# A two-block fp32 transformer kernel: the second block's streams and output products with sequence positions on the partitions

## What is computed

```python
for layer in range(DEPTH):                      # DEPTH = 2
    xm = modulate(h, g_pre_m, sh_m, sc_m)       # rms_norm_2(x, g) * (1 + scale) + shift
    cm = modulate(hc, g_pre_m, csh_m, csc_m)
    y, yc = even_mixer(...) or odd_mixer(...)   # each ends in ... @ w_out
    h = h + gt_m * rms_norm_2(y, g_post_m)
    f = conv_ffn(modulate(h, g_pre_f, sh_f, sc_f), w_up[layer], conv_w[layer], conv_b[layer], w_down[layer])
    h = h + gt_f * rms_norm_2(f, g_post_f)
    # layer 0 does the same two steps for hc
def conv_ffn(x, w_up, conv_w, conv_b, w_down):
    h = conv_over_sequence(x @ w_up) + conv_b   # 3 taps, each channel apart
    a, g = jnp.split(h, 2, axis=-1)
    return (jax.nn.silu(g) * a) @ w_down
```

## Time and profile before

| | us |
|---|---|
| median of three runs | 2123.23 |
| the three runs | 2123.23, 2120.9, 2126.95 |
| the profiled execution | 2119.83 |
| its span in the trace | 2117.8 |
| mean granted TensorE clock in it | 0.967 of full speed |

### The profile page before, as it was taken

The page is one execution under the profiler, slowest core; times in us unless marked ns, Lnnn a source line. Parts: engine busy times, 40 slices in busy tenths (PEclk is TensorE's granted clock), DMA queues, the critical chain, the costliest instruction groups (busy, mean ns, idle before and its releaser), DMA issues.

```text
span 2117.8 us, 33330 instructions
## 1 busy us (share of the span) xinstructions
PE 1988.5 (94%) x14346; PEld 1793.4 (85%) x14346; DVE 1186.1 (56%) x1541; ACT 948.9 (45%) x1294; POOL 12.9 (1%) x17
## 2 busy tenths in 40 slices
PE   6999889999999998899999989899999979979997
PEld 6998867998899887699979878788889978569997
DVE  5555774545544568654555473565553366746764
ACT  5434534434533453443455364543333255645553
POOL 0000000000000000000000100000000000000000
PEclk9999978999999999799999999899999999989998
DMA  7665534665466554476443220232232212023551
GB/s 284 251 219 199 179 126 153 249 229 210 168 233 233 210 174 174 151 271 239 148 162 117 100 80 21 73 104 102 81 101 97 100 60 97 24 80 117 183 192 68
DMA packets 45072, 320.90 MB, mean 152 GB/s; under 512 B 4992, under 2 KB 5120, under 8 KB 6400
## 3 DMA queue, kind: packets, MB, share of 16 engines
q1 hardware_dynamic: 38160, 270.09, 36.1%
q10 hardware_dynamic: 6768, 48.69, 6.2%
HBM read 317.72 MB, written 1.05 MB: 151 GB/s over the span
## 4 chain that ended last, share of the span: by engine, by line
PE 84%; DVE 8%; ACT 4%; issue 3%; DMA 0%; SPq 0%; DVEq 0%; ACTq 0%
PE ps L476 82%; DVE s_wl L1723 2%; ACT s_wh L1125 2%; DVE s_big L1993 1%; PE ps L769 1%; DVE s_tmp L2156 1%; ACT s_tmp L1401 1%; DVE s_tmp L1735 0%; PE ps L632 0%; DMA s_ca<-in_c_all 0%; PE ps L731 0%; DVE s_tmp L2112 0%; ACT s_xh L1404 0%; DVE s_X L1883 0%; ACT s_xh L1125 0%
## 5 line engine op out<-in xcount | busy, mean ns | idle before, releaser
L476 PE MATMUL ps<-s_xh,s_wl 128*128 128x256 f32 (+1 forms) x2400 | 734.2, 306 | 29.4 <-DVE s_wl L1723 15.8
L476 PE MATMUL ps<-s_xl,s_wh 128*128 128x256 f32 (+1 forms) x2400 | 725.7, 302 | 0.0
L476 PE MATMUL ps<-s_xh,s_wh 128*128 128x256 f32 (+1 forms) x2400 | 725.6, 302 | 0.0
L1723 DVE TENSOR_TENSOR s_wl<-s_raw,s_wh 128x2048 fp32r<-128x2048 f32 x215 | 492.3, 2291 | 404.3 <-ACT s_wh L1125 404.1
L476 PEld LDWEIGHTS ps<-s_xh,s_wl 128*128 128x128 f32 x2400 | 463.5, 193 | 50.0 <-DVE s_wl L1723 15.8
L1125 ACT ACTIVATE s_wh<-s_raw 128x2048 fp32r<-128x2048 f32 x215 | 409.5, 1906 | 191.0 <-PE ps L476 190.6
L476 PEld LDWEIGHTS ps<-s_xl,s_wh 128*128 128x128 f32 x2400 | 463.7, 193 | 15.6
L476 PEld LDWEIGHTS ps<-s_xh,s_wh 128*128 128x128 f32 x2400 | 463.1, 193 | 15.7
L476 PE MATMUL ps<-s_hh,s_wl 128*128 128x256 f32 x528 | 149.8, 284 | 0.0
L476 PE MATMUL ps<-s_hl,s_wh 128*128 128x256 f32 x528 | 149.4, 283 | 0.0
L476 PE MATMUL ps<-s_hh,s_wh 128*128 128x256 f32 x528 | 149.4, 283 | 0.0
(11 more groups left out here) (207 smaller groups left out, 2783.5 us busy)
## 6 DMA issues: line engine op xcount, KB each, us to landing
s_big<-in_w_ada ACTq DMA_DIRECT2D x46, 1024.0 KB, 6.6
s_raw<-in_ffn_gate SPq DMA_DIRECT2D x44, 1024.0 KB, 6.4
s_raw<-in_ffn_up SPq DMA_DIRECT2D x44, 1024.0 KB, 5.0
s_raw<-in_ffn_down SPq DMA_DIRECT2D x44, 1024.0 KB, 5.0
s_raw<-in_w_up SPq DMA_DIRECT2D x44, 1024.0 KB, 4.9
s_raw<-in_w_down SPq DMA_DIRECT2D x22, 1024.0 KB, 4.9
s_raw<-in_w_in SPq DMA_DIRECT2D x18, 1024.0 KB, 4.9
s_raw<-in_w_in_ab SPq DMA_DIRECT2D x10, 1024.0 KB, 4.9
```

Source lines behind the costliest of these rows:

```text
L476: return pe.matmul(o, lhsT, rhs, start=start, stop=stop, skip_group_check=True)
L1723: dve.tensor_tensor(wide(wl, u), raw[:, u % SLOTS, :].rearrange("p (k n) -> p k n", k=8), f32(wide(wh, u)), SUB).then_inc(*w_low.tick(u))
```

## The change

- **Layout.** The streams (`Xs`) and the products of output projection and conv down (`Ys`) have positions on the partitions: [128, 2, 1024]. The root mean square of a position is then a number of its partition.
- **Output projection** goes through `tokens`, in four pieces of 256 channels as before. **Conv down** (`conv_down`) takes the hidden stream as the stationary operand and 512 channels of a weight as columns: 8 x 3 products a step. The order of steps is the same.
- **Norms.** `bound_stat`, `bound_spread`, the sums and diagonals of squares are gone. ACT's Square accumulates along the row (`bound_squares`, `stream_squares`), DVE reduces a few columns, ACT takes the root, DVE the reciprocal, on 128x2.
- **Gain rows.** The gain (gate times g_post) must now be a row that is the same on all partitions. Six keys have one: "final", m00, m01, f00, f01, m10. DVE writes the gain's columns on diagonals (`gain_diagonals`, two of 128x512), PE spreads each with one fp32 product of 512 columns (`gains`), ACT copies the result out. DVE's `bound_evict` multiplies a bank by the row. The last conv down has no row: its gain is applied after a turn back.
- **Back for the projections.** `bound_turn` transposes the normed stream with four transposes for each of four parts; ACT applies scale and shift and makes the high part (`bound_high`), DVE does it again in full precision and subtracts (`bound_low`, three instructions a part).
- **Entry and end.** The context is transposed once, in four groups, in the down products of the last ffn2; modulation(1) stands earlier. At the end stream and product are both turned back, added in 8 instructions, and written by four DMAs of 256 KB where one of 1024 KB was.
- **Order and banks.** In the odd mixer all banks are renumbered by four, so the first projection u[0] writes bank 4; the weight part behind w_out_c unit 3 stands behind the chain and not ahead of it on ACT and DVE.

The gate of the even mixer on PE, before: the last gate product (four 128x128 from s_cb), ahead of the products of value(0).

The diff, cut to its core:

```diff
+        Xs = [by_token(X[:, q, :, :].rearrange("p k n -> p (k n)")) for q in range(2)]
+        Ys = [by_token(big[:, 2048 * q:2048 * q + 2048]) for q in range(2)]
...
-            def down(s, name, l, accs, streams_after, aside={}):
+            def conv_down(s, l, streams, aside={}):
...
-                        i = mm3(ps[b][:, 256 * (m % 2):256 * (m % 2) + 256], wide(wh, u)[:, k, at],
-                                wide(wl, u)[:, k, at], hh[:, n % 2, c], hl[:, n % 2, c],
-                                j == 0 and f == 0 and m % 2 == 0, end and f == 1)
+                        m = mm3(pair(ps[bank][:, :]), hh[:, n % 2, at:at + 128], hl[:, n % 2, at:at + 128],
+                                wide(wh, u)[:, c, :], wide(wl, u)[:, c, :], j + f == 0, j == 10 and f == 1)
...
+            def gains(key, banks):
+
+                for h, b in enumerate(banks):
+                    claim(b)
+                    pe.wait_ge(*gain_diag[key, h])
+                    mm(ps[b][:, :], const("mean256"), gain_diags[key][h], True, True).then_inc(
+                        *product.tick(("gain", key, h)))
+                    freed[b] = gain_row[key, h]
+
+            def bound_turn(B, *ps_):
+
+                for p in ps_:
+                    b = turn_bank[B][p]
+                    claim(b)
+                    pe.wait_ge(*normed[norm_of(B), p // 2 * 2 + 1])
+                    for t in range(2):
+                        for c in range(2):
+                            m = pe.transpose(ps[b][:, 256 * c + 128 * t:256 * c + 128 * t + 128],
+                                             Ys[B[2]][:, t, 256 * p + 128 * c:256 * p + 128 * c + 128], const("ident"))
+                    m.then_inc(*product.tick((norm_of(B), "turn", p)))
+                    freed[b] = x_low[norm_of(B), p]
...
-                    chunks(u, [n], [(B, "y", j)], 256, x_waits[q] if j < 2 else None, False, 256 * q,
-                           aside.get((j, q), {}), last=q == streams[-1])
+                    tokens(unit[name, j], [n], [(B, "y", j)], (2 * q, 2 * q + 1), x_waits[q] if j == 0 else None, False,
+                           aside.get((j, q), {}), last=q == streams[-1])
...
+                gains(("m", 0, 0), (4, 5))
                 value(0)
                 for n in range(len(H.units) + 3):
                     if n == 2:
                         value(1)
                     attend(H, n)
+                gains(("m", 0, 1), (6, 7))
...
-                    (1, 1): {6: lambda: bound_stat(B[0], 0, 0), 11: lambda: bound_spread(B[0], 0, 2)},
-                    (2, 1): {13: lambda: bound_stat(B[0], 1, 1)},
-                    (3, 1): {2: lambda: bound_spread(B[0], 1, 3)}})
+                    (2, 1): {10: lambda: bound_turn(B[0], 0, 1), 14: lambda: bound_turn(B[0], 2, 3)}})
...
+                    if j in aside:
+                        gains(aside[j], banks())
...
-                chunks(u[0], [0], [("odd", "q", 0)], 256, xw[0], True, 0, {
-                    5: lambda: bound_stat(P[1], 0, 4), 10: lambda: bound_spread(P[1], 0, 5)})
-                freed[0] = copied["odd", "q", 0]
+                chunks(u[0], [4], [("odd", "q", 0)], 256, xw[0], True, 0)
+                freed[4] = copied["odd", "q", 0]
...
+                       aside={1: step3, 9: step4, 17: step5, 20: lambda: gains(("m", 1, 0), (0, 1)), 23: lambda: attend(H, 0), 25: lambda: attend(H, 1)})
...
+            conv_ffn(0, (0, 1), {(0, 1): {11: lambda: bound_turn(M[1], 0, 1), 15: lambda: bound_turn(M[1], 2, 3)}},
+                     {3: ("f", 0, 0), 5: ("f", 0, 1)},
+                     {(21, 4): lambda: bound_turn(E, 0, 1), (21, 6): lambda: bound_turn(E, 2, 3)})
             odd()
...
+            bound_turn(("m", 1, 0), 0, 1, 2, 3)
+            conv_ffn(1, (0,), {}, {}, {})
...
+            def bound_squares(B, b, bank, earlier=None):
...
+                    for t in range(2):
+                        act.activation(T(b)[:, 256 * t:256 * t + 256], ps[bank][:, 256 * t:256 * t + 256], ACT.Square,
+                                       accum_out=bound(q, "y")[:, 4 * t + b:4 * t + b + 1]).then_inc(
+                                           *squared.tick((B, "y", b)))
...
+            def bound_evict(B, b, bank):
+
                 q = B[2]
...
+                dve.wait_ge(*squared[B, "y", b])
+                dve.wait_ge(*gain_row[B, 1])
...
+                    dve.scalar_tensor_tensor(out=half_of(Xs[q], b), in0=half_of(Ys[q], b),
+                                             scalar=bound(q, ("over", 0))[:, b % 2:b % 2 + 1], in1=half_of(Xs[q], b),
+                                             op0=MUL, op1=ADD).then_inc(*resid.tick((*B, b)))
...
+                    dve.wait_ge(*resid[(*B, b)])
+                    dve.tensor_scalar(half_of(Ys[q], b), half_of(Xs[q], b), bound(q, ("over", 1))[:, b % 2:b % 2 + 1],
+                                      None, MUL).then_inc(*normed.tick((norm_of(B), b)))
...
-            sp.wait_ge(*resid["f", 1, 0, 3])
-            sp.dma_start(out, X[:, 0, :, :]).then_inc(*out_done.tick(0))
-            sp.wait_ge(*out_done[0])
+            for p in range(4):
+                sp.wait_ge(*resid["out", p])
+                sp.dma_start(out[:, 2 * p:2 * p + 2, :], X[:, 1, 2 * p:2 * p + 2, :]).then_inc(*out_done.tick(p))
+            sp.wait_ge(*out_done[3])
```

683 lines of the change are left out of this document (397 added, 286 removed).

## The result

The changed kernel takes **2090.18 us** (median of four runs, 2087.8 to 2090.98), the kernel before 2122.07 (median of four, 2119.49 to 2126.95). The ratio is 0.9845, with a 95% interval of 0.9825 to 0.9865: 1.55% faster. The forecast was 2093.5 with a range of 2081 to 2108. The profiled execution of the changed kernel takes 2087.8 us with a span of 2085.8, so the span is shorter by 32.0 us; the sum had said 29.5.

What follows compares the result with a forecast made beforehand. PE products set most of the span, the rest being places where PE stands still. Savings of 55.0 less 25.5 added gave net 29.5, from 2119.83 to 2090.3; with 3.4 for the runs' median, 2093.5 us, range 2081 to 2108.

Steps and rivals of the forecast that it cites:

- (11): Gain key (m, 1, 0) at step 20 of u[5]: work 1.8 plus a 2.9 wait for diagonals, adding 4.7 us.
- (5): Odd mixer to conv FFN: pause from last product to restart falls from 22.75 to 11.0, saving 11.75 us.
- (6): End of program: 14.50 falls to 10.0, with 2.7 taken for the last DMA, saving 4.5 us.
- (1): Conv down, 33 steps: 512-column products take a step from 5.76 to 5.44, saving 9.9 us.
- (10): Gain keys (f, 0, 0) and (f, 0, 1) in the conv up: 4 x 0.9, adding 3.6 us.
- (2): Entry of block 2: four turns at 0.44 and 0.2 of waits remain of 4.3, saving 2.3 us.
- (3): Even mixer to conv FFN: stretch falls from 92.66 to 72.8, slack about 0.5 a quarter, saving 19.8 us.
- Rival B: Boundaries become bound by DVE, low parts 1.5 us late and the clock falling again: 2105; chance 0.2.
- (4): Conv down's end to odd mixer's projections: restart at 24.0 after DVE's bank 4 eviction, 50.8 against 57.6, saving 6.8 us.
- rival A: Gate wait costs nothing because attention's waits absorb it, or the odd entry's bank is free earlier: 2083; chance 0.2.
- (8): Gain key (m, 0, 0) ahead of value(0) waits for DVE's diagonals: 7.9 delay plus 2.5 clock, adding 10.4 us.
- C: Transposes let TensorE's clock fall at seven new places, some 2 us each, 14 in all: 2107; chance 0.04.

Runs made afterwards that it cites:

- the fill: 64 overwritten identity transposes in the pause behind the odd mixer's last product, added to the kernel with two gain-product moves and the earlier eviction: 2070.67 us.

## Why the prediction was right, point by point

**The sum.** The forecast's likeliest case came true, and every term but (11) lies within 0.8 us of the table; the total of the span is 32.0 against 29.5. Not every agreement was earned: in (5) and (6) it is partly luck.

**(1), (10).** Both rested on a row of the kernel before that had the new form in steady work (5.44 us a step, 0.9 a gain product), and they came out at 10.5 against 9.9 and at 3.5 against 3.6. The run with 256 columns shows that it is the products' shape and not the operand that is stationary.

**(2).** 3.1 against 2.3: PE is busy through the whole stretch of 31.27, so the 0.2 of waits and part of the 0.44 a turn were not there. Four transposes cost 0.40 among products.

**(3).** 73.61 against 72.8. The chain to the first turn takes 7.4 us in the trace, as worked out, and the 2.3 us of slack ahead of the turn were there (2.4); the run with the weight parts ahead shows that a delay has to use these up before PE waits. Rival B took each low part 1.5 us late against a slack of 0.5 us a quarter; in that run a delay of 3.1 cost 0.9.

**(4).** The restart came 24.3 us behind stream 0's last product (24.0 forecast), with the eviction as releaser, as it said. The part of rival A that had the bank free earlier did not happen by itself; the run that moves the eviction gets it.

**(5).** 11.26 against 11.0 for the pause, but two terms missed in opposite directions. Up to the turn the chain takes 7.2 us where the terms add up to 8.0; from the turn to the restart it takes 4.05 where they have 2.9. The terms took the turns and the parts behind them at full speed, while the transposes run at a granted clock of 0.50, so the first part reached ACT 1.1 us behind the start of the turn and not 0.5. With the fill, at full clock, the same stretch still takes 3.60, so 0.45 us of the 1.15 is the clock and the rest lies in the parts.

**(6).** 9.5 against 10.0. The transfer's 2.7 is now measured; the prediction had picked it between two bounds without a row, so that it fits is luck.

**(7), (9).** 3.7 and 2.4, for 3.8 and 3.0.

**(8).** Forecast 7.9 of delay and 2.5 of clock; the rows have 8.9 up to the start of value(0) and 1.7 more up to value(1), 10.7 together. The run with the products behind value(0) gives 9 back.

**(11).** 3.8 against 4.7: the wait is 1.84 and not 2.9.

**What the sum didn't have.** Two effects of the clock. Behind the odd mixer's end the stretch of 11.5 us had a granted clock of 0.94 where before it had 0.83, which gave 1.1 us back (the line of conv down, layer 1, in the table); the prediction had said that the half clock behind it stays. The likely reason is that PE does 16 transposes at the lower clock before the products start, where before it did a few small fp32 products with waits between; this was not tried apart. And in the odd mixer's statistics the same wait of 1.47 us for ACT that the kernel before has too was followed by a stretch at 0.73 (before: 1.00), which cost 1.5. The stretches, first of the changed kernel, then of the kernel before:

```profile
1754.20:1760.00 5.80, 5.80 (x38) 5.80 (x39) 1.17 (x4) 1.75 (x5) 0.00 (x0) 0.73 0.54 182
```

```profile
1770.00:1776.00 6.00, 6.00 (x55) 6.00 (x54) 2.21 (x6) 2.77 (x6) 0.00 (x0) 1.00 0.54 179
```

This is not the scatter of one execution: the clock falls there in the traces of all thirteen kernels that have the change (0.50 to 0.76 over 6 us), always behind the same 1.47. Why it didn't before stays open. The two effects nearly cancel, which is luck as well.

**The rivals.** A failed at the gate (9.8 us came back when the wait was taken away). B and D need waits that the trace doesn't show: in the stretch of (3) PE is busy all the time, and of the six gain keys only two wait for DVE, 5.94 and 1.84. C is refuted by the turns' stretches at 1.00 and by the fill with transposes.

## What to carry to other kernels

A helper product that waits for another engine's operand belongs behind the next product that needs nothing, and its read-out on the other engines belongs behind what they owe to the path. A bank that the next projection claims should be read out as early as the queue allows. Two moves of the first kind and one of the second gave 18.7 us. Before an edit is charged or credited, find which instruction on the releasing engine's queue stands in front, and how much slack there is: a delay of 3.3 us cost 3.3 at one boundary, one of 3.1 cost 0.9 at the other. For a new form of product, take the price from a row with that form in steady work.

## What the runs showed of the hardware

A step of 48 products of 256 columns takes 5.76 us, with the weight as the stationary operand (kernel before) and with the hidden stream (run with 256 columns); a step of 24 of 512 columns takes 5.44 with the hidden stream. One by one that is 0.120 and 0.227 us, and conv up's products of 512 columns, with a weight as the stationary operand, are 0.227 apart too. Transposes of fp32 tiles hold the granted clock at 1.00 through a pause of 7 us that without them brings it to 0.50 (1.2 GHz); 16 of them at the lower clock take 3.65 us, at the higher 1.94. The same wait of 1.47 us was followed by a clock of 1.00 in one kernel and of 0.73 in the other, and behind a wait of 1.84 us the same code had 1.00 in the traces of five kernels and 0.54 and 0.60 in those of two, so a short wait's price can't be read from its length alone. A last transfer of 256 KB behind three others takes 2.7 us to the end of the span, one of 1024 KB 4.3.
